# A hybrid layer on one core: u copied out of PSUM on ScalarE, q's first tile ahead of the transposed norm factors, two low parts and a scan moved forward

## The reference, cut to what matters

```python
hn = rms_norm(h, norm_mix)              # x * rsqrt(mean(x^2) + eps) * gain
proj = hn @ w_in                        # 1024 -> u (512), q (512), k (512), v (512)
u_ssm = proj[..., :512]
q, k = rms_norm(q, attn_qn), rms_norm(k, attn_kn)     # per head of 64
y_ssm = s5_mixer(u_ssm, ...)            # complex diagonal recurrence, 32 groups of 64 states
y_att = moba_attention(q, k, v, rel_bias)
h = h + concat(rms_norm(y_ssm), rms_norm(y_att)) @ w_out
h = h + memory_cross_attention(...)     # then a conv FFN with 2 x 2816 hidden channels
```

## Time and profile before

| | us |
|---|---|
| median of 3 runs | 669.65 (669.63 to 670.72) |
| the profiled execution | 670.81 |
| its span | 668.8 |
| PE busy in the span | 656.2 (98%) |
| DVE busy | 487.2 (73%) |
| ACT busy | 340.6 (51%) |
| POOL busy | 172.5 (26%) |

### The profile page before, as it was taken

The page is one execution under the profiler, slowest core; times in us unless marked ns, Lnnn a source line. Parts: engine busy times, 40 slices in busy tenths (PEclk is TensorE's granted clock), DMA queues, the critical chain, the costliest instruction groups (busy, mean ns, idle before and its releaser), DMA issues.

```text
span 668.8 us, 10548 instructions
## 1 busy us (share of the span) xinstructions
PE 656.2 (98%) x3914; PEld 542.1 (81%) x3914; DVE 487.2 (73%) x801; ACT 340.6 (51%) x587; POOL 172.5 (26%) x177
## 2 busy tenths in 40 slices
PE   8899999999999999999999999999999999999997
PEld 7688778877888788887998888888888888888886
DVE  5998998578766665557697666666656687868967
ACT  6538564766745464764354333334334345554662
POOL 4998992223220102330000111011110121100000
PEclk9999999999999999999999999999999999999999
DMA  8868515666120404030357555564566446655663
GB/s 296 309 206 130 167 44 145 177 185 221 64 66 1 158 2 188 4 124 0 127 189 249 199 182 188 192 225 151 186 222 218 151 170 223 211 189 140 182 196 125
DMA packets 67737, 106.99 MB, mean 160 GB/s; under 512 B 15792, under 2 KB 40496, under 8 KB 66288
## 3 DMA queue, kind: packets, MB, share of 16 engines
q1 hardware_dynamic: 64528, 100.17, 45.9%
q10 hardware_dynamic: 3168, 6.29, 2.9%
HBM read 89.54 MB, written 15.73 MB: 157 GB/s over the span
## 4 chain that ended last, share of the span: by engine, by line
PE 80%; DVE 11%; ACT 3%; SPq 2%; DMA 2%; issue 1%; POOL 1%; ACTq 0%; DVEq 0%
PE pb L510 23%; PE pb L512 23%; PE pb L511 23%; PE pb L1962 6%; PE pb L1965 4%; DVE F L1384 3%; DVE wring L500 2%; ACT F L993 1%; DMA raw<-in_w_in 1%; SPq L664 1%; DMA F<-scr_y 1%; DVE F L1390 1%; DVE pb L1384 1%; DVE sq L1432 1%; DVE wring L1384 1%
## 5 line engine op out<-in xcount | busy, mean ns | idle before, releaser
L510 PE MATMUL pb<-xs,wring 128*128 128x512 f32 (+1 forms) x400 | 149.6, 374 | 0.7 <-POOL xs L911 0.7
L512 PE MATMUL pb<-xs,wring 128*128 128x512 f32 (+1 forms) x400 | 148.9, 372 | 0.0
L511 PE MATMUL pb<-xs,wring 128*128 128x512 f32 (+1 forms) x400 | 148.9, 372 | 0.0
L1390 DVE SCALAR_TENSOR_TENSOR F<-pb,cols,F 128x511 f32<-128x511 f32 x88 | 65.9, 748 | 71.6 <-ACT F L993 69.7
L500 DVE TENSOR_TENSOR wring<-raw,wring 128x1024 fp32r<-128x1024 f32 x70 | 93.4, 1336 | 8.0 <-ACT wring L489 7.9
L510 PE MATMUL pb<-wring,xs 128*128 128x512 f32 x240 | 98.5, 411 | 0.3 <-DVE wring L503 0.3
L993 ACT ACTIVATE F<-pb,cols 128x512 f32<-128x512 f32 x50 | 38.2, 767 | 115.3 <-PE pb L512 115.2
L512 PE MATMUL pb<-wring,xs 128*128 128x512 f32 x240 | 93.9, 391 | 0.0
L511 PE MATMUL pb<-wring,xs 128*128 128x512 f32 x240 | 93.7, 390 | 0.0
L510 PEld LDWEIGHTS pb<-xs,wring 128*128 128x128 f32 x400 | 75.3, 188 | 14.1 <-issue 1.3
L512 PEld LDWEIGHTS pb<-xs,wring 128*128 128x128 f32 x400 | 75.3, 188 | 13.2
(11 more groups left out here) (152 smaller groups left out, 1011.1 us busy)
## 6 DMA issues: line engine op xcount, KB each, us to landing
raw<-in_ffn_w_up SPq DMA_DIRECT2D x22, 1024.0 KB, 5.3
F<-in_ffn_w_down SPq DMA_DIRECT2D x11, 1024.0 KB, 4.9
scr_w<-F SPq DMA_DIRECT2D x11, 1024.0 KB, 3.9
F<-in_x SPq DMA_DIRECT2D x8, 512.0 KB, 8.6
raw<-in_w_in ACTq DMA_DIRECT2D x4, 1024.0 KB, 6.3
raw<-in_w_out SPq DMA_DIRECT2D x4, 1024.0 KB, 4.9
raw<-scr_w SPq DMA_DIRECT2D x8, 512.0 KB, 3.8
raw<-scr_w SPq DMA_DIRECT2D x15, 256.0 KB, 4.7
```

Source lines behind the costliest of these rows:

```text
L510: nc.tensor.matmul(ps, lh, rh, start=first, stop=False)
L511: nc.tensor.matmul(ps, lh, rl_, start=False, stop=False)
L512: return nc.tensor.matmul(ps, ll, rh, start=False, stop=last)
L1390: return V.scalar_tensor_tensor(out=o, in0=a, scalar=s1, in1=b, op0=o1, op1=o2)
```

## The change

It does five things. (1) u is copied out of PSUM by ACT, unscaled and in the same regrouped order, ahead of `xb`. (2) DVE multiplies these copies by `xbc` inside SBUF, in place; piece 0 after `turns(0)`, pieces 1 to 3 after `turns(1)`. A new semaphore `u_ready` counts the scaled pieces; SP's `u_write(q)` waits for it, and so does ACT where it waited for bank 3's drain. (3) Both low parts of q's first chunk (units 4 and 5) come right after `mean_sq("x")`, ahead of `root`; `turns(0)` moves behind `root`. (4) On PE the wait for `xr_ready` and the four transposes stand behind tile 0 of unit 4 instead of inside u's last product. (5) `scan(1)` comes ahead of low part 11. Nothing else moves: ACT's queue from `split_hi(act, 7)` on and POOL's program are as before.

```diff
--- before.py
+++ after.py
@@ -211,6 +211,7 @@
 
         raw_in = [sem("raw_in0"), sem("raw_in1")]
         piece_in = [sem(f"piece_in{i}") for i in range(len(PIECES))]
+        u_ready = sem("u_ready")
         k_hi, u_hi, u_lo, x0_in = sem("k_hi"), sem("u_hi"), sem("u_lo"), sem("x0_in")
         x_in = [sem(f"x_in{t}") for t in range(TT)]
         mem_in, memt_in = sem("mem_in"), sem("memt_in")
@@ -642,7 +643,7 @@
                 sync.dma_start(memr[:, t, :], A["mem"][0, t * 128:(t + 1) * 128, :]).then_inc(mem_in, 16)
 
             def u_write(q):
-                after_drain(sync, f"u{q}")
+                sync.wait_ge(u_ready, q + 1)
                 sync.dma_start(scr_u[q * 128:(q + 1) * 128].rearrange("p i k -> p (i k)"), uT[:, q, :])\
                     .then_inc(su_out if q else su0_out, 16)
 
@@ -1039,6 +1040,8 @@
             split_hi(act, U_Q + 1)
             by_step = lambda a: a.rearrange("p (k i) -> p i k", i=L)
             steps_first = lambda a: a.rearrange("p (i k) -> p i k", i=L)
+            for m in range(4):
+                drained(A_(steps_first(uT[:, m, :]), by_step(read(act, f"u{m}")[:, :]), ACT.Copy), f"u{m}")
             drained(A_(steps_first(xbc), by_step(read(act, "xb")[:, :]), ACT.Copy), "xb")
             split_hi(act, U_Q + 2)
             act.wait_ge(mem_in, 16 * MT)
@@ -1115,7 +1118,7 @@
             kernels_in(0)
             load_chunk(act, 5)
             split_hi(act, 9)
-            after_drain(act, "u3")
+            act.wait_ge(u_ready, 4)
             rows("q", qk)
             split_hi(act, 10)
             inv_root("q")
@@ -1533,23 +1536,22 @@
             dve.wait_ge(sq_done, TT)
             mean_sq("x")
             dve.wait_ge(pw_ready, 1)
+            split_lo(dve, U_Q)
+            split_lo(dve, U_Q + 1)
+            root("x", xr_ready)
             turns(0)
-            root("x", xr_ready)
-            split_lo(dve, U_Q)
-
-            def u_evac(m):
-
-                by_step = lambda a: a.rearrange("p (k i) -> p i k", i=L)
-                steps_first = lambda a: a.rearrange("p (i k) -> p i k", i=L)
-                p = read(dve, f"u{m}")
+
+            def u_scale(m):
+
+                after_drain(dve, f"u{m}")
                 if m == 0:
                     after_drain(dve, "xb")
-                drained(tt(steps_first(uT[:, m, :]), by_step(p[:, :]), steps_first(xbc), ALU.mult), f"u{m}")
-
-            for m in range(4):
-                u_evac(m)
+                tt(uT[:, m, :], uT[:, m, :], xbc, ALU.mult).then_inc(u_ready, 1)
+
+            u_scale(0)
             turns(1)
-            split_lo(dve, U_Q + 1)
+            for m in range(1, 4):
+                u_scale(m)
             split_lo(dve, U_Q + 2)
             turns(2)
             split_lo(dve, U_Q + 3)
@@ -1614,8 +1616,8 @@
             head_event("q", qk, range(TT), H, "q")
             split_lo(dve, 10)
             head_rows("q", qk, range(TT), H, HD)
+            scan(1)
             split_lo(dve, 11)
-            scan(1)
             split_lo(dve, 12)
             dve.wait_ge(gain_in, 16)
             b = COL["ssm_b_glu"]
@@ -2037,13 +2039,14 @@
                             last = u_pass(m, k, a)
                         if k == KD - 1:
                             filled(last, f"u{m}")
-                            if m == 1:
-                                pe.wait_ge(xr_ready, 1)
-                                token_factors("xb", "x")
                 if k0 + n in (2, 4, 6):
                     last.then_inc(unit_used, 1)
 
-            proj(4, U_Q, "q")
+            for t in range(TT):
+                proj_tile(4, U_Q, "q", t)
+                if t == 0:
+                    pe.wait_ge(xr_ready, 1)
+                    token_factors("xb", "x")
             def weights_in(q):
 
                 pe.wait_ge(w1p_ready, q + 1)
```

## The result

| | before | after |
|---|---|---|
| median, us | 669.96 (669.63 to 670.72, 4 runs) | 677.77 (677.14 to 678.44, 4 runs) |
| the profiled execution | 670.81 | 677.9 |
| its span | 668.8 | 676.1 |
| PE, DVE, ACT, POOL busy | 656.2, 487.2, 340.6, 172.5 | 656.9, 488.2, 343.2, 168.9 |

The change makes the kernel slower: the ratio is 1.0115, with a 95% interval of 1.0098 to 1.0133. The forecast was 677.3. Lines of the changed kernel stand one to four further down: low parts are L501, DVE's general two-input operation L1387, ACT's L994, transposes L1967.

A forecast was written before the change was run, and what follows sets the result against it. PE, busy 656.2 of 668.8 us, bounds the kernel. ACT's queue +7.1 less 0.92 gives +6.1; with clock 1.6, +7.7: profiled 670.81 becomes 678.5, and 1.16 lower for the median 677.3 us, range 675.5 to 680.

The forecast's parts named there:

- PE's start: From u to q on PE: hole, slow clock and bank 0 wait gone, 4.3 us gained, nearly all lost at unit 6.
- DVE's chain, +2.0: DVE up to the sines: u's multiplications take turns with POOL, so ACT's first sine begins 2.0 us later.
- The 2.0 us reach `kernels_in(1)`: From the sines to `kernels_in(1)`: no hole between, so this stage also comes 2.0 us later and PE waits there.
- the one at 82: PE's wait for ACT at q's third transposes, from 82.0 to 87.2; the first hole's clock loss comes out of it.
- ACT's queue, +7.1 at the third transposes: Chunk 7's load waits for low part 11, holding `qt_evac(0)`; PE starts q's third transposes at 87.2, 7.1 us later.
- Rival 3: ACT's queue doesn't matter, the turns do: +2.0 less 0.92, +1.1 us, 670.7, no difference; chance 5%.
- The 0.9 us of `scan(1)` at `outputs(1)`: PE's wait of 0.92 us for `scan(1)` ahead of `outputs(1)` goes away with the scan ahead of low part 11.
- The clock, 1.6: After PE's stop at q's third transposes the lower clock costs 1.6 us, with ends 0.7 and 2.8.
- What follows is tied to it: After q's third transposes PE has no stop for over 50 us, so the later work is tied to that delay.

The follow-up runs named there:

- The row in PSUM: The changed kernel with the factors' row left in PSUM, read there by DVE, and ACT's copy of it dropped: 678.18 us, ratio 1.0125.
- the second profile: Profile of the changed kernel run once more, unaltered: median 678.79 us, ratio 1.0133.
- the run with the load moved: The changed kernel with chunk 7's load moved behind the four evacuations of q's transposes in ACT's queue: 671.45 us, ratio 1.0017.
- the start alone: The changed kernel with low part 11 ahead of `scan(1)` again: 672.58 us, ratio 1.0036.
- the scan alone: The kernel before with `scan(1)` ahead of low part 11 and nothing else: 675.93 us, ratio 1.0078.
- the repeated best version: Second run of the kernel before with `scan(1)` ahead of low part 11 and chunk 7's load behind q's evacuations: 669.35 us, ratio 0.999.
- the one with three more waits: The kernel before with `scan(1)` early and chunk 7 loaded later, plus three repeated, long-met waits at u's multiplications: 669.01 us, ratio 0.9983.
- the first run of the best version: The kernel before with `scan(1)` ahead of low part 11 and chunk 7's load behind q's evacuations: 669.15 us, ratio 0.9986.
- chunk 7 later alone: The kernel before with chunk 7's load behind the evacuations of q's transposes and nothing else: 670.19 us, ratio 1.0003.

## Why the prediction was right

The sum was 677.3, the result 677.77. By its own steps:

- **PE's start: right.** Predicted: no hole, factors ready at 31.4, unit 6 stopped from 42.2 to 46.1. Measured: 0.51 us at 31.38, clock 1.00 there, a stop to 46.01. The 4.3 us of gain up to the eight transposes is real and is worth nothing.
- **DVE's chain, +2.0: right.** The first sine began at 53.82, predicted 53.8. The low part of unit 6 ended at 45.95, predicted 46.1. The ten ends of POOL's instructions that the prediction lists all came within 0.2 us. The row in PSUM shows the cause.
- **The 2.0 us reach `kernels_in(1)`: right.** PE waits 1.23 there and starts at 70.73; before it started 2.0 sooner and waited 0.4. The low clock behind 46 us cost nothing, as forecast, but it was paid out of this wait and not out of the one at 82 that the forecast named.
- **ACT's queue, +7.1 at the third transposes: right in kind, short by 0.9 in the first profile** (88.12 instead of 87.2), since q's heads took a microsecond more; in the second profile it was 87.42. Rival 3, by which the queue didn't matter, is refuted by the run with the load moved.
- **The 0.9 us of `scan(1)` at `outputs(1)`: right.** It is gone in the change and is gained outright once the queue is clear.
- **The clock, 1.6: mis-sized for the first profile, though within its stated ends (0.7 and 2.8).** From the third transposes to `outputs(1)` PE took 6.48 us, before 3.85 without its wait (84.91 less 80.14 less 0.92): 2.6 lost. In the second profile it was 1.4.
- **"What follows is tied to it": wrong in part, and this hid the misses.** `outputs(1)` began 9.7 us late, the span grew by 7.3. The kernel before has four small stops of PE between 140 and 158 us:

```profile
140.01 0.50 PE L510 MATMUL pb<-wring,bs 128*128 128x512 f32 x1 [0.19 <-ACT F L993]
142.22 0.49 PE L1962 MATMUL pb<-F 64*128 64x128 f32 x4 [0.55 <-ACT pbuf L993]
...
156.62 0.44 PE L1962 MATMUL pb<-F 128*64 128x128 f32 x4 [0.34 <-DVE F L396]
157.74 0.47 PE L510 MATMUL pb<-xs,wring 128*128 128x512 f32 x1 [0.68 <-POOL xs L911]
```

They sum to 1.76 us, and the changed kernel's first profile has none of them. With PE up to 5.8 us late (the start alone, the scan alone, the row in PSUM) they stand nearly unchanged; with 7.8, in the second profile, the first two are gone, with 9.7 all. It looks as if the other engines catch up only when PE is held long enough.

So two misses, 0.9 + 1.0 us too little and some 1.8 to 2.4 too much, cancel in the first profile. In the second, `outputs(1)` came 7.8 us late, against a sum of 7.7, without such help; but here too 1.2 us of it were given back later (the span grew by 6.6), and the median of that run lay 8.9 above the kernel before on its chip. That the total hit within 0.5 us is partly luck; that the kernel would be slower by this mechanism is not.

## What to carry to other kernels

Before moving an instruction later, ask which semaphore it raises and what stands behind the first waiter in that engine's queue: here a transfer that nobody needed for long waited for a low part, and held four evacuations for which PE stood. When an order change costs more than the moved instruction, move the waiter as well; both edits together gained where one alone lost 5.6 us. And a hole closed on the bound engine is worth only what the next tie leaves of it: follow the chain that feeds the engine, not the engine.

## What the runs showed of the hardware

- **The clock after a hole isn't a fixed price.** Behind a stop of PE at 31 us the granted clock fell to 0.50 in the kernel before (2.59 us), in the repeated best version (2.54) and in the one with three more waits (3.21), and stayed at 1.00 in the first run of the best version (3.17), with chunk 7 later alone (3.12) and with the scan alone (2.21). These two rows of windows, around the same place, are of the version with three more waits and of the first best run:

```profile
32.00:34.00 2.00, 2.00 (x7) 1.54 (x6) 1.69 (x4) 2.00 (x3) 1.92 (x2) 0.58 0.02 4
```

```profile
32.00:34.00 2.00, 1.85 (x10) 1.24 (x9) 1.69 (x3) 1.51 (x3) 1.92 (x2) 1.00 0.00 0
```

  And behind the stop of 5 to 6 us the slow stretch lasted until 94 us in one profile of the change and until 91 in the other.
- **Two instructions more went with a microsecond at the program's end**, when they put a packet of code beside the last transfer: 2.8 to 2.9 us of waiting instead of 1.8, in three kernels, undone by taking out three waits that were long met.
- **DVE and POOL can fall into step in two ways.** The same four multiplications of q's heads took 5.66 or 6.67 us in two executions of one program. POOL's instruction that starts with them (L871) took 1.84 us in the first case and 1.27 in the second, so it was held where they were not.
